# Block sums of the weights moved from GpSimd to VectorE, with one buffer and one split per engine, in the Strassen MLP of a hybrid decoder layer

## The reference

```python
def _channel_and_ple(h, mix, p_l, w_out, g_ffn, w_up, w_down, w_ple, w_ple_norm, w_ple_gate):
    h = h + mix @ w_out
    u = _rmsnorm(h, g_ffn)
    h = h + jnp.square(jax.nn.relu(u @ w_up)) @ w_down
    e = _rmsnorm(p_l @ w_ple, w_ple_norm) * jax.nn.sigmoid(h @ w_ple_gate)
    return h + e
```

## Time and profile before

| | us |
|---|---|
| median of 3 runs | 2873.52 (2872.86 to 2875.92) |
| the profiled execution | 2880.84 |
| its span, first to last instruction | 2879.1 |
| TensorE busy | 2587.6 (90%) |
| VectorE busy | 1942.9 (67%) |
| POOL busy | 1852.0 (64%) |
| ScalarE busy | 1025.7 (36%) |

### The profile page before, as it was taken

The page is one execution under the profiler, slowest core; times in us unless marked ns, Lnnn a source line. Parts: engine busy times, 40 slices in busy tenths (PEclk is TensorE's granted clock), DMA queues, the critical chain, the costliest instruction groups (busy, mean ns, idle before and its releaser), DMA issues.

```text
span 2879.1 us, 49824 instructions
## 1 busy us (share of the span) xinstructions
PE 2587.6 (90%) x20223; PEld 2455.9 (85%) x20223; DVE 1942.9 (67%) x2160; ACT 1025.7 (36%) x1343; POOL 1852.0 (64%) x1466
## 2 busy tenths in 40 slices
PE   7999999966767998799999999988989898997998
PEld 7999999923346998799999999888989898987998
DVE  4277777628468225687877787887878787888433
ACT  3111111238643214443434444433434333333222
POOL 0098999200045205799999999988888888873322
PEclk9999999988877999899999999999999999998999
DMA  4388888398721333344444444543333333331223
GB/s 130 114 279 267 282 301 288 117 379 344 262 81 59 111 118 112 106 143 148 146 140 147 143 145 141 173 137 107 114 110 112 111 111 111 111 103 44 89 92 115
DMA packets 316425, 442.16 MB, mean 154 GB/s; under 512 B 16269, under 2 KB 267851, under 8 KB 315022
## 3 DMA queue, kind: packets, MB, share of 16 engines
q1 hardware_dynamic: 276600, 384.49, 40.4%
q10 hardware_dynamic: 39598, 54.50, 5.8%
HBM read 402.16 MB, written 36.88 MB: 152 GB/s over the span
## 4 chain that ended last, share of the span: by engine, by line
PE 41%; POOL 27%; DVE 19%; DMA 6%; issue 3%; ACT 3%; SPq 1%; POOLq 0%; ACTq 0%; DVEq 0%
PE ps L1415 7%; PE ps L1417 7%; PE ps L1420 7%; PE ps L1823 5%; PE ps L1824 5%; PE ps L1825 5%; POOL wsum L1290 5%; POOL raw L1291 5%; POOL kpage L1217 4%; POOL wsum L1294 4%; POOL wsum L1293 4%; DVE wc L2397 3%; DVE wc L2395 3%; DMA kpage<-in_cache_k 2%; DMA raw<-in_w_up 1%
## 5 line engine op out<-in xcount | busy, mean ns | idle before, releaser
L1823 PE MATMUL ps<-opl_h,wc 128*128 128x260 f32 x2296 | 667.1, 291 | 59.5 <-DVE acc L2465 47.0
L1824 PE MATMUL ps<-opl_l,wc 128*128 128x260 f32 x2296 | 663.6, 289 | 0.0
L1825 PE MATMUL ps<-opl_h,wc 128*128 128x260 f32 x2296 | 662.4, 289 | 0.0
L2395 DVE TENSOR_TENSOR wc<-raw,wc 128x1024 fp32r<-128x1024 f32 x256 | 372.9, 1457 | 252.0 <-ACT wc L997 250.4
L1415 PE MATMUL ps<-uh,wh 128*128 128x260 f32 x1952 | 515.9, 285 | 16.6 <-DVE wl L1943 14.0
L997 ACT ACTIVATE wc<-raw 128x1024 fp32r<-128x1024 f32 x256 | 271.6, 1061 | 701.6 <-PE ps L1825 509.0
L1417 PE MATMUL ps<-ul,wh 128*128 128x260 f32 x1952 | 512.6, 284 | 0.0
L1823 PEld LDWEIGHTS ps<-opl_h,wc 128*128 128x128 f32 x2296 | 448.2, 195 | 67.2 <-issue 56.8
L1943 DVE TENSOR_TENSOR wl<-raw,wh 128x1024 fp32r<-128x1024 f32 (+1 forms) x162 | 258.6, 1597 | 343.0 <-ACT wh L724 342.8
L1217 POOL TENSOR_TENSOR kpage<-kpage,qbc 128x1024 f32<-128x1024 f32 x128 | 357.1, 2824 | 157.6 <-DMA kpage<-in_cache_k 157.5
L1824 PEld LDWEIGHTS ps<-opl_l,wc 128*128 128x128 f32 x2296 | 448.6, 195 | 0.0
(11 more groups left out here) (419 smaller groups left out, 4986.4 us busy)
## 6 DMA issues: line engine op xcount, KB each, us to landing
kpage<-in_cache_k SPq DMA_DIRECT2D x128, 512.0 KB, 4.9
vpage<-in_cache_v SPq DMA_DIRECT2D x128, 512.0 KB, 6.0
raw<-in_w_up SPq DMA_DIRECT2D x128, 512.0 KB, 3.6
raw<-in_w_down SPq DMA_DIRECT2D x128, 512.0 KB, 3.4
raw<-in_w_in SPq DMA_DIRECT2D x88, 512.0 KB, 4.7
hid_scr<-hout ACTq DMA_DIRECT2D x32, 520.0 KB, 3.4
hst<-hid_scr ACTq DMA_DIRECT2D x32, 520.0 KB, 3.5
raw<-in_w_out SPq DMA_DIRECT2D x32, 512.0 KB, 3.4
```

Source lines behind the costliest of these rows:

```text
L1823: mm(out, h_, xh, start=first and q == 0, stop=False)
L1824: mm(out, h_, xl, start=False, stop=False)
L1825: z = mm(out, l_, xh, start=False, stop=last and q == 1)
L2395: tt(w_[:, 1, 0:1024], raw3[s % 3], w_[:, 0, 0:1024].bitcast(F32), ALU.subtract).then_inc(lo_ready, 1)
```

## The change

The sums of the weights move from POOL to VectorE, as three instructions of 512, 256 and 256 elements: `w_s31` (S3 = A21 - A11 and, in place, A21 - A22, in one instruction that reads A21 twice) and `w_s24` (S2, then S4, which waits for S2). Signs and the order of products change to fit. Raw blocks and sums lie in one buffer `wr` of seven blocks per q, three of them, with high parts in `wch` and low parts in `wcl`, so ScalarE and VectorE split each slab in one instruction of 1792 elements. The load of a slab is two DMAs, one per q. VectorE's order in window w is now: `relu`, `w_s31(w+3)`, `w_lo(w+2)`, `gather_x`, `w_s24(w+3)`, `combine`, `hidden_lo`, `gather_y`.

The staging buffer and T1 to T4 become one buffer `ob` of eight halves, `t_sums` has three instructions in place of four, and a hidden block is split by one instruction per engine (`hidden_hi`, `hidden_lo`, 1820 elements). `combine` has six steps in place of seven. POOL keeps `t_sums` and `state_step`, and no longer waits for anything per slab. To make room, the last block of `hT` moves (`h15`), its stores are two DMAs per pair, `rstd` swaps its halves, and POOL's clearing of `acc` comes after the MLP. The diff, cut to its core:

```diff
-PRODUCTS = [(RAW_A11, 512, O_B11, 4), (SUM_S2, 128, O_T2, 5), (SUM_S3, 128, O_T3, 6), (RAW_A12, 512, O_B21, 0),
-            (SUM_S4, 128, O_B22, 1), (RAW_A22, 512, O_T4, 2), (RAW_A21, 512, O_T1, 3)]
+W_S3, W_A11, W_A21, W_A12, W_A22, W_S2, W_S4 = range(7)
+P1, P6, P7, P2 = (W_A11, O_B11, 4), (W_S2, O_T2, 5), (W_S3, O_T3, 6), (W_A12, O_B21, 0)
+P3 = (W_S4, O_B22, 1)
+UP_PRODUCTS = [P1, P6, P7, P2, P3, (W_A21, O_T1, 2), (W_A22, O_T4, 3)]
+DOWN_PRODUCTS = [P1, P6, P7, P2, P3, (W_A22, O_T4, 2), (W_A21, O_T1, 3)]
...
             def load_w(s):
...
-                sp.dma_start(raw3[s % 3].rearrange("p (k n) -> p k n", k=4), w_rows(s)).then_inc(w_in_[s % 3], 16)
+                rows = w_rows(s)
+                for q in range(2):
+                    half = wr[s % 3][:, q, W_A11:W_A22 + 1].rearrange("p (m c) n -> p m (c n)", m=2)
+                    sp.dma_start(half, rows[:, 2 * q:2 * q + 2]).then_inc(w_in_[s % 3], 16)
...
             def w_hi(s):
                 if s >= 2:
                     act.wait_ge(w_used, SL_MLP + 2 * (s - 2) + 2)
-                act.wait_ge(*w_sum.at(2 * s + 1))
-                A(wc[s % 3][:, 0, 0:1024], raw3[s % 3], ACT.Copy).then_inc(hi_ready, 1)
-                act.wait_ge(*w_sum.at(2 * s + 2))
-                A(wc[s % 3][:, 0, 1024:], wsum[s % 2].rearrange("p a q n -> p (a q n)"), ACT.Copy)\
-                    .then_inc(hi_ready, 1)
+                act.wait_ge(*w_sum.at(3 * s + 3))
+                A(wch[s % 3], wr[s % 3], ACT.Copy).then_inc(hi_ready, 2)
...
+            def hidden_hi(p):
+                act.wait_ge(*o_t.at(8 + p + 1))
+                A(ring[p % 5][0], ob[:, 1:8], ACT.Copy).then_inc(o_h.sem, 2)
...
             def hidden_load(p):
 
-                act.wait_ge(*o_l.at(2 * (8 + p) - 1))
-                act.wait_ge(*o_t.at(8 + p))
+                act.wait_ge(*o_l.at(2 * (8 + p)))
                 act.wait_ge(*v_out[p % 2].at(16 * (p // 2 + 1)))
-                act.dma_start(hst, hid_scr[p]).then_inc(o_in.sem, 16)
+                act.dma_start(ob[:, 0:4], hid_scr[p]).then_inc(o_in.sem, 16)
...
-            def w_sums(s):
-
-                pool.wait_ge(w_in_[s % 3], 16 * (s // 3 + 1))
-                if s >= 2:
-                    pool.wait_ge(lo_ready, SL_MLP + 2 * (s - 1) + 2)
-                v = raw3[s % 3].rearrange("p (q n) -> p q n", q=2)
-                a11, a21, a12, a22 = [v[:, :, o:o + P] for o in (RAW_A11, RAW_A21, RAW_A12, RAW_A22)]
-                s2, s3, s4 = [wsum[s % 2][:, x] for x in range(3)]
-                pool.tensor_tensor(s3, a11, a21, ALU.subtract)
-                pool.tensor_tensor(a21, a21, a22, ALU.add).then_inc(w_sum.sem, 1)
-                pool.wait_ge(*w_sum.at(2 * s + 1))
-                step(pool.tensor_tensor(s2, a21, a11, ALU.subtract))
-                pool.tensor_tensor(s4, a12, s2, ALU.subtract).then_inc(w_sum.sem, 1)
...
-                step(pool.tensor_tensor(tsum[:, 0], b12, b11, ALU.subtract))
-                step(pool.tensor_tensor(tsum[:, 1], b22, tsum[:, 0], ALU.subtract))
-                pool.tensor_tensor(tsum[:, 2], tsum[:, 1], b11, ALU.subtract)
-                pool.tensor_tensor(tsum[:, 3], b21, tsum[:, 1], ALU.subtract).then_inc(o_t.sem, 1)
+                step(pool.tensor_tensor(ob[:, 4], ob[:, 0], ob[:, 1], ALU.subtract))
+                step(pool.tensor_tensor(ob[:, 5:7], ob[:, 2].unsqueeze(1).to_broadcast([P, 2, HALF]), ob[:, 0:5:4],
+                                        ALU.add))
+                pool.tensor_tensor(ob[:, 7], ob[:, 3], ob[:, 6], ALU.subtract).then_inc(o_t.sem, 1)
...
             for w in range(1, ALL_SLABS):
-                if w + 3 < ALL_SLABS:
-                    w_sums(w + 3)
...
+            def w_s31(s):
+                v = wr[s % 3]
+                dve.wait_ge(w_in_[s % 3], 32 * (s // 3 + 1))
+                tt(v[:, :, W_S3:W_A12:2], v[:, :, W_A21:W_A12].to_broadcast([P, 2, 2, P]), v[:, :, W_A11:W_S2:3],
+                   ALU.subtract).then_inc(w_sum.sem, 1)
+
+            def w_s24(s):
+                v = wr[s % 3]
+                dve.wait_ge(*w_sum.at(3 * s + 1))
+                tt(v[:, :, W_S2], v[:, :, W_A11], v[:, :, W_A21], ALU.subtract).then_inc(w_sum.sem, 1)
+                dve.wait_ge(*w_sum.at(3 * s + 2))
+                tt(v[:, :, W_S4], v[:, :, W_A12], v[:, :, W_S2], ALU.subtract).then_inc(w_sum.sem, 1)
+
             def w_lo(s):
-                w_ = wc[s % 3]
-                dve.wait_ge(hi_ready, SL_MLP + 2 * s + 1)
-                tt(w_[:, 1, 0:1024], raw3[s % 3], w_[:, 0, 0:1024].bitcast(F32), ALU.subtract).then_inc(lo_ready, 1)
                 dve.wait_ge(hi_ready, SL_MLP + 2 * s + 2)
-                tt(w_[:, 1, 1024:], wsum[s % 2].rearrange("p a q n -> p (a q n)"), w_[:, 0, 1024:].bitcast(F32),
-                   ALU.subtract).then_inc(lo_ready, 1)
+                tt(wcl[s % 3], wr[s % 3], wch[s % 3].bitcast(F32), ALU.subtract).then_inc(lo_ready, 2)
...
             def combine(g):
...
+                tt(ho[:, 1], ut[:, 0], bank(0), ALU.add).then_inc(v_d.sem, 1)
+                tt(ut[:, 0], ut[:, 0], bank(5), ALU.add).then_inc(v_d.sem, 1)
                 dve.wait_ge(*v_d.at(n + 2))
+                tt(ut[:, 1], ut[:, 0], bank(6), ALU.add).then_inc(v_d.sem, 1)
                 dve.wait_ge(*v_p.at(b + 6))
...
+                tt(ut[:, 0], ut[:, 0], bank(2), ALU.add).then_inc(v_d.sem, 1)
+                dve.wait_ge(*v_d.at(n + 4))
+                tt(ho[:, 0], ut[:, 0], bank(1), ALU.add).then_inc(v_d.sem, 1)
                 dve.wait_ge(w_used, SL_MLP + 2 * (4 * g + 4) + 2)
...
+                tt(ho[:, 2:4], ut[:, 1].unsqueeze(1).to_broadcast([P, 2, HALF]), ps[:, 2:4, 0:HALF], ALU.add)\
+                    .then_inc(v_d.sem, 1)
...
             for w in range(ALL_SLABS):
+                ends = w >= UP_SLABS and DOWN_AT[w - UP_SLABS][4]
+                if 4 <= w <= UP_SLABS and w % 4 == 0:
+                    relu(w // 4 - 1)
+                if w + 3 < ALL_SLABS:
+                    w_s31(w + 3)
                 if w + 2 < ALL_SLABS:
                     w_lo(w + 2)
...
+                if ends:
+                    i, n = DOWN_AT[w - UP_SLABS][0:2]
+                    gather_x(i, n)
+                if w + 3 < ALL_SLABS:
+                    w_s24(w + 3)
...
+                for p in range(PAIR):
+                    if w == prep_window(p):
+                        hidden_lo(p)
+                if ends:
+                    gather_y(i, n)
                     if n < 4 and i == LAST_ROUND[n]:
                         finish_h(n)
```

More of the change, by code:

```diff
@@ L194, in build @@
         hrc = const("hrc", [QB])
+        rstd_at = cpos[0]
+        rstd = const("rstd", [T])
         dtt_at = cpos[0]
@@ L965, in square @@
                 act.wait_ge(h_a, c + 1)
-                A(sqo, hT[:, 2 * c:2 * c + 2, :], ACT.Square).then_inc(h_q, 1)
+                if c < 7:
+                    A(sqo, hT[:, 2 * c:2 * c + 2, :], ACT.Square).then_inc(h_q, 1)
+                else:
+                    A(sqo[:, 0], hT[:, 14], ACT.Square)
+                    A(sqo[:, 1], h15, ACT.Square).then_inc(h_q, 1)
             def store_h(g):
-                act.dma_start(h_scr[g], hT[:, 2 * g:2 * g + 2, :]).then_inc(hs_out, 16)
+                for m in range(2):
+                    act.dma_start(h_scr[g, :, m], h_of(g)[m]).then_inc(hs_out, 16)
             def stage(k):
@@ L1040, in p1_copy @@
                 if g:
-                    act.wait_ge(*v_d.at(8 * g))
+                    act.wait_ge(*v_d.at(7 * g - 2))
+                else:
+                    act.wait_ge(hs_out, 32 * 8)
                 A(ut[:, 0], ps[:, 4, 0:HALF], ACT.Copy).then_inc(v_m.sem, 1)
             def hidden_square(g):
-                act.wait_ge(*v_d.at(8 * g + 8))
+                act.wait_ge(*v_d.at(7 * g + 7))
                 A(hout[g % 2], hout[g % 2], ACT.Square).then_inc(v_m.sem, 1)
@@ L1333, in _ @@
             for w in range(1, ALL_SLABS):
-                if w + 3 < ALL_SLABS:
-                    w_sums(w + 3)
                 if w == 1:
                     t_sums(7)
-                if w == 3:
-                    pool.wait_ge(h_rt, 2)
-                    step(pool.memset(acc, 0.0))
                 for k in range(3):
@@ L1346, in _ @@
                         t_sums(8 + p)
+            pool.wait_ge(*h_fin.at(4))
+            pool.wait_ge(h_rt, 2)
+            step(pool.memset(acc, 0.0))
             for g in range(8):
@@ L1808, in norm_sum, with strassen @@
                 last.then_inc(h_s, 1)
-            def strassen(s, ops, first, last, bank_free):
+            def strassen(s, products, ops, first, last, bank_free):
                 pe.wait_ge(lo_ready, SL_MLP + 2 * s + 4)
-                w_ = wc[s % 3]
-                for x, (off, qstep, o, bank) in enumerate(PRODUCTS):
+                for x, (wb, o, bank) in enumerate(products):
                     if first:
@@ L1876, in _ @@
                 pe.wait_ge(*o_l.at(2 * (8 + pairs[1] + 1)))
```

(37 more changed lines are left out.)

140 lines of the change are left out of this document (61 added, 79 removed).

## The result

The changed kernel takes 2905.47 us (median of four runs, 2902.46 to 2908.58) against 2874.72 for the kernel before on the same chip: a ratio of 1.010, 95% interval 1.008 to 1.012. It is slower by 1%, where I had forecast 0.2% faster. The time lies inside the range given (2808 to 2918), the direction was wrong.

The account below looks back on a forecast made before the run. TensorE, busy 90% of the span, was taken to lose time to POOL's late sums in the weight path. Start -5, w_up +27, turn and end 0, w_down -28 sum to -6 us: 2867.5 us, range 2808 to 2918.

Parts of the forecast that it names:

- The loop and its order: MLP: ScalarE's split, VectorE's split and two sums run in series, 4.61 us per slab against TensorE's 5.04.
- VectorE starts 0.04 after it: Loop hand-overs between ScalarE and VectorE: the waiting engine starts 0.04 us after the end, within a turn of 4.61 us.
- Group ends: w_up, every 4 slabs: VectorE's combination makes the group 20.97 us against 20.15, 0.82 late, 25 us in all.
- State steps: w_up: eight sets on POOL delay VectorE's loop by 5.0 us each, 40 us in all.
- rival C: Clock falls at stalls in w_down and at state steps: +50 us, so 2917; chance 0.22, nearly all slower.
- w_down: Steady w_down: 45.3 us per eight slabs against 47.6, including 2.1 for POOL's operand sums, twelve times: -28 us.
- Turn and end at 0: Turn to w_down and end of the MLP: no change, with 5 us either way.
- Start: Slabs 0 to 3: ScalarE's 4.00 us wait for POOL goes, VectorE gains sums; -5 us, bounds -15 and +6.
- B: Rival: the loop has slack and POOL's delays to VectorE miss it, about 2814 us; chance 0.22, all faster.
- D: Rival: weight path not freed, half loads land late and VectorE waits at w_s31; +128, about 2995 us; chance 0.06.
- A: The forecast itself, the loop sets the pace: 2867.5 us, spanning 2845 to 2892; chance 0.50.
- The rule on semaphores: If followed, a turn takes 4.50 us and the 25 us of w_up's group ends vanish: 2842 us; not adopted.

Follow-up runs that it names:

- e6: Changed kernel with only the waits of the two loop hand-overs changed (splits add 1, ScalarE's wait for the sums first): 2888.3 us, 1.0043 of the kernel before.
- e2: Changed kernel with the three POOL instructions of each of the eight state steps cut to 1 of 128 columns: 2866.54 us.
- e3: Changed kernel with POOL's three operand sums per hidden block cut to 8 of 260 columns: 2865.74 us.
- e5: Number not assigned in the text; apparently the changed kernel with ScalarE's split adding 1, the other increment given before it: 2903.49 us.
- e9: Number not assigned in the text; apparently the changed kernel with one extra 240-element VectorE instruction per w_up window, in the idle place: 2912.7 us.
- e10: Number not assigned in the text; apparently the changed kernel with the same extra 240-element VectorE instruction per w_up window, inside the loop: 2945.43 us.
- e1: Changed kernel with one line moved, w_s24(w+3) right behind w_s31(w+3) and ahead of w_lo(w+2): 2822.7 us, 0.981 of the kernel before.

## Why the prediction was wrong, point by point

*The loop and its order* were right: POOL gone from the chain, ScalarE waiting for `s4`, VectorE for ScalarE, w_up slower, w_down faster, `w_lo` 2.02 and the sums 0.69, 0.42, 0.42. The strided and repeated operands cost nothing extra, and 1792 elements on ScalarE took 1.70 where I had 1.72.

*The failed step, first part: "VectorE starts 0.04 after it"*, used for both hand-overs of the turn. I took it from the row of a single instruction with its wait on board and applied it to instructions that the diff gives an increment of 2. They took 0.11 and 0.12, so the turn is 4.75 instead of 4.61. Three plain turns a group: 30 x 3 x 0.14 = 12.6 us, as much as the miss in w_up (39.7 - 27 = 12.7). The turn through the group's end had 7.14 in my sum (11.75 less 4.61) and has 7.14. e6 shows the mechanism and its size per turn: with the short hand-overs w_up is 686, where I had forecast 685.

*The failed step, second part: the terms put at nothing.* The hand-over alone doesn't turn the sign back. e6 has it at 0.03 us and takes 2888 us, still 0.4% more than the kernel before. Against the forecast it lies over by 2.4 us in the turn (114.1 less 111.8), 4.3 in the end (97.2 less 92.9), 4.0 in w_down (547.5 less 543.5) and 2.5 at the start. So the miss is made of the hand-over, 17 us by e6, and of the loop in the turn and end, the operand sums and the start; and a sign that hung on 6 us was not safe against any of them. Some 9 us of the measured 30.75 are the place of the two profiled executions among their runs.

*Group ends*: forecast 0.82 us each, 25 in all for 30. In e2, by slab, 28 of them come to 34.1 us, 1.22 each, the first two are on pace, and slab 120, also behind a group's end, has 4.2. The difference of 0.40 is the same 0.14 three times. At slab 120 GpSimd forms the first hidden block's operand sums, which my sum for w_up left out (the stretch of that slab in e2):

```profile
1790.90:1800.20 9.30, 6.88 (x44) 6.67 (x43) 9.16 (x13) 1.70 (x1) 2.27 (x2) 0.82 0.18 56
```

So part of the match between 12.6 and 12.7 is luck too: the group ends measure 9 us over their term, slab 120 adds 4, the state steps are 0.6 under theirs.

*State steps*: forecast 8 x 5.0 = 40, measured 39.4 (e2). The size was right, but by luck. TensorE's idle time accounts for (697.0 - 643.5) - (657.6 - 628.2) = 24.1 of it, and 15.3 are longer busy time for the same matmuls (643.5 against 628.2), with the granted clock at 0.97 against 1.00, which I had left to rival C. One such place, slab 24 with its group end (stretch of the changed kernel):

```profile
1284.50:1296.70 12.20, 7.45 (x43) 7.26 (x43) 12.03 (x16) 1.70 (x1) 2.32 (x1) 0.72 0.13 43
```

4.8 us of stall, and 7.5 us for 43 matmuls that take 5.1 otherwise, at a granted clock of 0.72.

*w_down*: without operand sums I had 43.2 us per eight slabs, and e3 gives 43.8 (525.2 / 12); with them 45.3, and it is 46.1 (552.7 / 12). So the term of 2.1 us for them measures 2.3, and the other 0.6 us are the base of the period, of which e6 gives back 0.4 (552.7 less 547.5, over 12) with the hand-overs alone. That is near what can be told: in runs that leave w_down as the change has it (e2, e5, e9, e10) the stretch took 553.1 to 556.6 us. Periods differ; an undisturbed one and another:

```profile
2125.80:2171.00 45.20, 41.49 (x336) 40.55 (x337) 41.74 (x47) 16.87 (x10) 6.67 (x6) 1.00 0.37 118
2032.90:2080.20 47.30, 43.16 (x337) 42.12 (x336) 42.55 (x47) 16.86 (x10) 5.92 (x7) 0.96 0.35 113
```

In the second the longest stall is 2.2 us and the clock is 0.96. What I had not seen is where the gain comes from. TensorE's idle time in w_down is 50.3 us (552.7 - 502.4) against 51.4 before: the stalls did not shrink at all. They were cut up, the 4 us pieces are gone, and the busy time for the same matmuls fell from 520.1 to 502.4, clock 0.93 to 0.99. So 17.7 of the 18.8 us gained are busy time, not waiting. Busy time measures the clock only roughly: in e3 w_down has a granted clock of 1.00 and 497.45 us busy, 13.6 over the pace of 96 x 5.04.

*Turn and end at 0*: they measured +2.9 and +6.0. I had no reason to hold the loop out of them; both are made of the same windows. In e1's order they take 109.3 and 94.0, and in e3, without the operand sums, the turn takes 106.4.

*Start*: -2.2 of -5; ScalarE's wait for the sums did not go, it is 3.6 us long and now for VectorE. Nothing was tried on it.

*The rivals*: B (delays miss the loop) fell with e2. C was half right. Its 30 us in w_down did not come, the clock there rose; its 20 us at the state steps did in the main, as the 15.3 us of e2. Against the kernel before, w_up's busy time rose by 11 us (632.35 to 643.49) and its clock fell from 0.99 to 0.97; how much of the 11 is clock isn't shown, since e2 has 8.6 us over pace at a clock of 1.00. D did not come. I had given "slower" 0.41 in all (0.14 in A, 0.21 in C, 0.06 in D), and the sign hung on two terms of 27 and 28 us, which missed by 12.7 and 9.2. That both miss upward comes in part from their common source, the turn (11.0 and 5.2 us by e6).

The rule on semaphores that I weighed (the Trainium skill, "VectorE: DVE Perf Modes", "The DRAIN you can't avoid": one after each instruction costs nothing extra) I had refused by a wrong reading. All the instructions compared add to a semaphore, and the independent ones start 0.35 us apart all the same (1332.67 to 1333.02, and 0.34 in rows 7), so the semaphore itself costs nothing in these rows: the trace agrees with the rule. What costs 0.11 us is to wait for the step just before (0.45, 1332.22 to 1332.67), which that rule doesn't price; so it gave no reason to take the 25 us of the group ends away. Nor does it speak of how a wait is issued, which is what e6 prices.

What one could have done better without a chip: the turn had 0.43 us of slack by my sum and the order of three lines decided it. Writing the loop down and then asking which of its members need to be in it leads to e1 directly: `w_s24(w+3)` doesn't need `w_lo(w+2)`.

## What to carry to other kernels

When work moves to another engine, write down the circle that its new place closes (who waits for whom, once around) and move out whatever doesn't need to be inside; 83 us lay in one line here, while VectorE's busy time hardly changed. Test a suspected loop by putting one small instruction inside it and the same one beside it. Before crediting a change with taking an engine off the path, take away the work that makes that engine late: in w_up the sums were never late by themselves, the state steps were, and they cost as much from outside the path.
